# Two weight buffers of a two-block transformer kernel placed 64 bytes further on in on-chip memory

## What is computed

```
h = rms_norm(x, norm1_w)
(rq, rk, rv, rg, dq, dk, dv, cb, cc, cx, gates) = [h @ w_in[:, s:e] for s, e in column_bounds()]
...            # retention, differential attention, short convolution
merged = (g[:, :, 0] * (ret @ w_branch[0]) + g[:, :, 1] * (diff @ w_branch[1])
          + g[:, :, 2] * (conv @ w_branch[2]))
x = x + merged @ w_out
u = jnp.square(jax.nn.relu(rms_norm(x, norm2_w) @ w_up))
return x + u @ w_down
...            # second block: stick-breaking attention, gated linear attention,
               # and a gated feed-forward of width 2816 with a short convolution
```

## The kernel before

| buffer | start modulo 256 | remark |
|---|---|---|
| `xh`, `xl`, `bh`, `bl` | 128 | rows of 576 elements, 2304 bytes = 9 x 256, so every chunk begins at 128 |
| `wraw`, `wh`, `wl` | 128 | 8192 bytes each; a chunk is 512 bytes, so every chunk and slot begins at 128 |
| `qq`, `kk`, `vt`, `mrg`, `res` and their float32r twins, `xrows` | 128 | the sums read in L2295 begin there |

## Time and profile before

### The profile page before, as it was taken

The page is one execution under the profiler, slowest core; times in us unless marked ns, Lnnn a source line. Parts: engine busy times, 40 slices in busy tenths (PEclk is TensorE's granted clock), DMA queues, the critical chain, the costliest instruction groups (busy, mean ns, idle before and its releaser), DMA issues.

```text
span 2115.3 us, 33898 instructions
## 1 busy us (share of the span) xinstructions
PE 2102.7 (99%) x13662; PEld 1854.7 (88%) x13662; DVE 1242.1 (59%) x1847; ACT 830.8 (39%) x1305; POOL 165.3 (8%) x146
## 2 busy tenths in 40 slices
PE   9999999999999999999999999999999999999998
PEld 8998888888888788898898888999999998889897
DVE  6774444564555555767664666367855557456364
ACT  4333222433444443434434566343424343222233
POOL 0012000030000000232120000022300000000000
PEclk9999999999999999999999999999999999999999
DMA  4343221522222333332323221231133222322322
GB/s 150 110 171 108 85 76 60 198 81 80 74 68 71 100 101 99 107 110 80 109 90 93 86 92 53 88 121 59 53 143 100 90 80 90 99 90 91 98 90 99
DMA packets 53563, 203.36 MB, mean 96 GB/s; under 512 B 6960, under 2 KB 7344, under 8 KB 52288
## 3 DMA queue, kind: packets, MB, share of 16 engines
q1 hardware_dynamic: 49248, 177.56, 26.1%
q10 hardware_dynamic: 3232, 20.80, 2.5%
q0 software_dynamic: 960, 3.24, 0.5%
HBM read 190.96 MB, written 10.62 MB: 95 GB/s over the span
## 4 chain that ended last, share of the span: by engine, by line
PE 93%; DVE 4%; ACT 2%; issue 0%; DMA 0%; SPq 0%; DVEq 0%; ACTq 0%
PE ps L2172 69%; PE ps L2295 7%; PE ps L2771 6%; PE ps L2637 1%; PE ps L2419 1%; PE ps L2444 1%; PE ps L2372 1%; PE ps L2703 1%; PE ps L2543 1%; DVE kk_r L1825 1%; PE ps L2458 1%; ACT kk L964 1%; ACT kk L965 1%; PE ps L2681 0%; PE ps L2524 0%; PE ps L2351 0%
## 5 line engine op out<-in xcount | busy, mean ns | idle before, releaser
L554 ACT ACTIVATE wh<-wraw 128x1024 fp32r<-128x1024 f32 x284 | 300.0, 1056 | 742.7 <-PE ps L2172 626.1
L1232 DVE TENSOR_TENSOR wl<-wraw,wh 128x1024 fp32r<-128x1024 f32 x298 | 367.2, 1233 | 136.4 <-ACT wh L554 132.4
L2172 PE MATMUL ps<-xh,wh 128*128 128x264 f32 (+1 forms) x1800 | 326.3, 326 | 0.6 <-DVE tmp L1265 0.5
L2172 PE MATMUL ps<-xl,wh 128*128 128x264 f32 (+1 forms) x1800 | 318.9, 322 | 0.0
L2172 PE MATMUL ps<-xh,wl 128*128 128x264 f32 (+1 forms) x1800 | 318.5, 322 | 0.0
L2172 PEld LDWEIGHTS ps<-xh,wh 128*128 128x128 f32 x1800 | 265.0, 188 | 30.8 <-issue 2.4
L2172 PEld LDWEIGHTS ps<-xh,wl 128*128 128x128 f32 x1800 | 265.2, 188 | 26.7
L2172 PEld LDWEIGHTS ps<-xl,wh 128*128 128x128 f32 x1800 | 265.3, 188 | 26.7
L2172 PE MATMUL ps<-bh,wh 128*128 128x264 f32 (+1 forms) x1296 | 233.1, 324 | 0.3
L2172 PE MATMUL ps<-bh,wl 128*128 128x264 f32 (+1 forms) x1296 | 229.8, 321 | 0.0
L2172 PE MATMUL ps<-bl,wh 128*128 128x264 f32 (+1 forms) x1296 | 229.6, 321 | 0.0
(11 more groups left out here) (532 smaller groups left out, 2778.1 us busy)
## 6 DMA issues: line engine op xcount, KB each, us to landing
wraw<-weights_dram SPq DMA_DIRECT2D x299, 512.0 KB, 3.5
qq<-weights_dram SPq DMA_DIRECT2D x12, 512.0 KB, 4.1
kk<-weights_dram SPq DMA_DIRECT2D x12, 512.0 KB, 4.5
hf<-tables_dram POOLq DMA_DIRECT2D x12, 264.0 KB, 3.1
res<-x_t_dram SPq DMA_DIRECT2D x4, 528.0 KB, 7.2
res<-x_t_dram ACTq DMA_DIRECT2D x1, 2112.0 KB, 9.2
res_dram<-res ACTq DMA_DIRECT2D x1, 2112.0 KB, 6.4
mrg_dram<-mrg ACTq DMA_DIRECT2D x1, 2112.0 KB, 8.7
```

Of the source, the lines that this page charges most:

```text
L554: nc.scalar.activation(wh[:, slot], wraw[:, slot], ACT.Copy).then_inc(hi_done, 1)
L1232: nc.vector.tensor_tensor(wl[:, slot], wraw[:, slot], wh[:, slot].bitcast(F32), ALU.subtract)\
L2172: last = nc.tensor.matmul(o, w[:, slot, c, :], a[:, c, tok], start=(k == 0), stop=(k == len(steps) - 1))
```

## The change

`sb(name, shape)` allocates a buffer of float32 behind the last one. Two buffers that nothing reads or writes are added, 64 bytes ahead of `wh` and `wl` and 192 bytes behind them:

```diff
         wraw = sb("wraw", [P, 2, KC, P])
+        sb("ahead_of_weights", [P, 16])
         wh, wl = sb("wh", [P, 2, KC, P], F32R), sb("wl", [P, 2, KC, P], F32R)
+        sb("behind_weights", [P, 48])
         qq, qqr = shared("qq", [P, KC, T])
```

## The result

The changed kernel takes 2102.31 us (median of 4 runs, 2102.25 to 2102.43) against 2116.98 us for the kernel before on the same chip (2116.91 to 2117.26): a ratio of 0.9931, with a 95% interval of 0.9913 to 0.9948. It is 14.7 us faster, where the prediction had it 11.5 us slower.

The account below looks back on a forecast made before the run. PE, busy 99% of the span, bounds the kernel: number of matmuls times the distance between starts. Terms of +11.0 and +0.5 us summed to +11.5 us on 2117.05 us, giving 2128.5 us, range 2105 to 2141 us.

Parts of the forecast that it names:

- The step that failed: In L2333, two matmuls with both operands at 192 read some 234 ns each, so distance 0 was taken as dear.
- 512-column strips: 3,288 matmuls in strips, distance 64 to 0: from 229.95 to 233.3 ns each, +11.0 us.
- L2771: 528 matmuls of 512 columns, distance 192 to 0: dear both, 0; -2.3 us if they fell to 229.0 ns.
- 264 columns: 6,384 matmuls in L2172 and L2586, distances 0 and 32 to 192 and 224: stay at 120.1 ns, 0.
- L2295: 300 matmuls with `xh` or `xl` moving go from 118.3 to 120.0 ns, +0.5 us; sums stay at 120.0.
- ACT, DVE and DMA: Copies into shifted `wh` and `wl` stay covered by PE work; DMA into `wraw` keeps place and size: 0.
- the two readings: Either the distance between moving and stationary starts decides a matmul's cost, or the moving start by itself; distance was favoured.
- The rival "nothing": The moving start alone sets the level, or the stationary address does not enter: 2117.0 us; chance 0.22.
- The faster rival: 264-column matmuls of L2172 and L2586 fall to 118.3 ns, 512-column ones stay: -10.9 us, 2106.1 us; chance 0.17.

Follow-up runs that it names:

- the run with the pair at 64: Kernel before, with the stationary operand of L2333's three pairs starting at element 64 instead of 16 (distance 64 instead of 0): 2116.11 us against 2117.12.

## Why the prediction was wrong

**The step that failed** is the sentence that distance 0 "reads as dear at 512 columns as it does at 256", taken from L2333 in the earlier trace rows: 234 ns for two matmuls with both operands at 192. The same two matmuls, addresses and all, take 226 ns each in the changed kernel. They came out of strips in the 226, 229, 232 cycle, and what I read as their level was two steps of a transition. That the stretch of 219 behind them stood at 233.3 ns I read as a sign of their own cost; it was their effect on the matmuls that followed, which the run with the pair at 64 shows. A pair of matmuls cannot show the level of a distance when three are needed to settle. The other half of the sentence was true: at 256 columns distance 0 is dear, 120.0 ns where all of L2297 lies at it (rows 64 bytes lower), against 117.9 on average where `xh` and `xl` had distance 64 before. What failed was carrying that order over to 512 columns, where distance 0 measures 226.7 ns, the lowest level of all. Term by term:

- *512-column strips:* forecast +11.0 us, measured -8.3. The forecast had a rise of 4.3 ns from 229.0 to 233.3; measured is a fall to 226.7, by 2.3 ns from 229.0 and by 6.6 from 233.3. At distances 32, 48 and 192, which cost 233.3, the same sum would have been right: the run with the weights 128 bytes on has +10.7 us there.
- *L2771:* forecast 0 ("dear both"), measured -3.4 us (123.52 to 120.17), 233.3 to 226.7 ns, by the same error. Its bound had been the cycle's 229.0; the level of 226.7 stood in no long stretch before.
- *264 columns:* forecast 0, measured -0.7 us, by indifference to 192 and 224 as to 0 and 32. This term was right, and the warning that each nanosecond there is 6.4 us was worth giving: at 128 and 160 it is +14.5 us. Two figures beside it were off without touching the sum: 120.1 ns is 9.2% over the bare 110, not 7.6%, and the cost on top of the bare clock was 10 to 20 ns in the rows shown, not 7 to 20.
- *L2295:* forecast +0.5, measured -2.5 us. `xh` and `xl` on `wh` and `wl` did get dearer (118.1 to 119.05 ns; 120.0 in the third pass). But the sums on distance 192, left at 120.0, fell to 116.1, and matmuls whose addresses stayed fell from 117.9 to 115.3 behind them. Costing each matmul by its own distance left that out.
- *ACT, DVE and DMA:* 0, as measured (1057 and 1228 ns).

**The choice between the two readings** of the earlier trace rows was right for shifts of 64 bytes: the distance decides and not the moving start alone, since rows moved down or weights moved up brought strips and L2771 to the same 226.7 ns, and moving everything by 64 bytes gave a ratio of 1.0000. At 16 bytes the distance alone is not enough. The rival "nothing" falls: between 2102.2 and 2139.6 us the instructions are the same and only addresses differ. That the weight load is the other party is an inference from the fact that the stationary start matters; no run here had matmuls without loads beside them. The Trainium skill (page "TensorE: Matmul & The Clock Gate", "Step-by-step: what each phase is for") says that loading the next tile's weights does not steal SBUF read bandwidth from the running matmul. The unchanged 2117.0 us that I had drawn from it did not come; whether the sentence itself fails here hangs on that inference.

**The faster rival** had the outcome and not the cause: its place was the 264-column matmuls, which gave 0.7 of 14.7 us, while the 512-column strips, which it left as they were, gave 8.3.

**What stays open.** Why 16 bytes are cheap one way for strips and the other way for L2771; why distance 0 is the cheapest at 512 columns, dear at 256 and one of several equals at 264; why 233.3 ns at distance 64 in two stretches behind L2295; and what makes the levels at all.

## What to carry to other kernels

Where TensorE is busy throughout and each weight tile serves one or two matmuls, measure the distance between starts in long undisturbed stretches and compare it with columns over clock: a few per cent over it may be a matter of where the two operands begin. Pad rows so that the distance stays the same from chunk to chunk, and try a few shifts with unused buffers. The same start modulo 256 bytes is the first to try for 512 columns; at 264 it gave nothing and at 256 it was dear. The cheap window is narrow and its neighbours can cost more than it gives (here from -0.7% to +1.1%). Don't read a level off a handful of matmuls: what ran before them decides it.

## What the runs showed that I had not expected

- Several long-run means come in even steps. 120.0, 226.7 and 233.3 ns are 18, 34 and 35 times 6.67 ns (16 periods of the 2.4 GHz clock); the cycle of 226, 229, 232 is 103 times that for three matmuls, and 113.3 ns, which 256 columns reach in the changed kernel, is 17 times. Others, such as 232.6 and 122.3 ns, are no whole multiples. No run tells why.
- TensorE carries a level on. In one stretch two matmuls at distance 0 ahead of 219 at distance 64 made the difference between 228.9 and 233.3 ns for each of the 219.
- The cheap distance hangs on the width: 0 is the cheapest at 512 columns (226.7 ns) and dear at 256 (120.0 ns).
- Two buffers that hold nothing are worth between -14.7 and +22.6 us in a kernel whose instructions, granted clock and traffic stay the same.
